# Moving a decoder's activation tiles and split weight buffers by some tens of columns in SBUF

## The chip, the cores and the metric

The kernel runs on one NeuronCore of a Trainium2 chip. The metric is the device time of one execution in microseconds (us), lower is better. Before the change it was 1270.6 us, the median of three runs (1267.6 to 1275.32).

## The reference

Three transformer blocks are computed on 256 tokens of width 1024, in float32. Cut to what matters:

```python
def first_block(x, mem, ...):
    for i in range(2):
        hn, mn = _rmsnorm(x, norm1[i]), _rmsnorm(mem, norm_mem[i])
        if i == 0: mix, q_mem = _nsa_mixer(hn, nsa_w_in, ...)      # sparse attention, 12 heads
        else:      mix, q_mem = _rwkv7_mixer(hn, rw_w_in, ...)     # recurrence over the tokens
        cross = _mem_attention(q_mem, mn, w_mem_kv[i])             # 256 memory rows
        x = x + jnp.concatenate([mix, cross], -1) @ w_o[i]
        x = x + _swiglu(_rmsnorm(x, norm2[i]), w_ffn_in[i], w_ffn_out[i])
    return _rmsnorm(x, final_norm)

def second_block(x, ...):
    proj = rmsnorm(x, mix_pre_g) @ w_in                            # 1024 -> 7176
    y_a = spatial_gating(...); y_b = forgetting_attention(...)
    x = x + rmsnorm((sigmoid(g_a) * y_a + sigmoid(g_b) * y_b) @ w_out, mix_post_g)
    return x + rmsnorm(swiglu(rmsnorm(x, ffn_pre_g), w_gate, w_up, w_down), ffn_post_g)
```

All weights together are some 180 MB, and each is used once.

## The kernel before

**Products.** Each large float32 product is made from three matmuls in the type float32r: both operands are split into a high part (`hi`) and the rest (`lo`), and `product` (L796) issues hi·hi (L798), then two mixed terms (L799, L800), into one PSUM bank. Each matmul loads its own stationary operand (LDWEIGHTS, the rows PEld) beside the matmul that runs before it.

**Weights.** SP loads them in pieces of 1024 columns by 256 outputs (2048 columns of 4 bytes in each of 128 partitions, `SLOT`) into a ring of three slots. ACT copies a piece into `w_hi` (L1622) and DVE writes the rest into `w_lo` (L2079). `w_hi` and `w_lo` have two slots each (`SPLITS`); piece number m goes to slot m mod 2. `split(name, k)` (L787) gives a piece's two views to PE. ACT fills a slot again when PE has done the piece before it there.

**Activations.** The normalised activations lie transposed, feature by token, in `act_hi` and `act_lo`, eight tiles of 256 tokens each (`KT` tiles of `S`). Together they are `fm` (L207). Every stage that begins with activations writes them into `fm` (`from_banks`, L1583 on ACT and L2036 on DVE) and reads them from there. The hidden layer of the three feed-forward parts has its own `hT_hi`, `hT_lo`, and the memory rows theirs (`mem_fm`, L285).

**Units.** PE goes through units in a fixed order. `fm_unit` (L802) has weights as the stationary operand and 256 tokens as the moving one; `tm_unit` (L821) has 128 tokens as the stationary operand and 256 columns of weights as the moving one; a full unit of either is 48 matmuls. `row_unit` (L850) has tokens as the stationary operand and 512 columns of weights as the moving one, 24 matmuls a piece. The stages, in order, with their matmuls through `product`:

| stage | what | units | matmuls |
|---|---|---|---|
| nsa | inputs of the sparse attention | q0 to qm0, most fm, two tm | 504 |
| mem | keys and values of the memory rows | kmem, vmem | 192 |
| wo0 | output projection | row | 96 |
| f0 | feed-forward: 22 fm units, then 11 row units on hT | f0_in, f0_out | 1056 + 264 |
| z | inputs of the recurrence | z0 to z10, qm1, fm | 552 |
| wo1, f1 | as wo0, f0 | | 96, 1056 + 264 |
| b2 | inputs of the second block | sv, fv, su, ga, gb are tm, fq, fk, sf fm | 1368 |
| wo2, f2 | as wo0, f0 | | 96, 1056 + 264 |

Between z and wo1 stands the recurrence itself (small matmuls of 64 by 64 in plain float32). There `cms` and `tt` (L311, L332) borrow the room of the activations, and `sc_parts`, `ems` (L294, L309) that of the split weights.

**Addresses.** `place` (L155) puts one tensor behind another, each start a multiple of 8 columns (a column is 4 bytes in each partition). `act_hi` begins at column 8192 and `act_lo` at 10240 of the kernel's room. The arena, which starts with `w_hi`, begins at column 24304. Since 16112 = 24304 − 8192 is 48 more than a multiple of 64, and all tile and slot sizes are multiples of 64, every tile of weights starts 48 columns (mod 64) behind every tile of activations. `hT` and the memory rows lie at a multiple of 64 from the weights.

```python
act_hi = place("act_hi", KT * S, dtype=F32R)             # L168
act_lo = place("act_lo", KT * S, dtype=F32R)             # L170
W_HI, W_LO = 0, SPLITS * SLOT                            # L192
fm = (tiles(act_hi), tiles(act_lo))                      # L207
pe.matmul(o, ahl[0], bhl[0], start=first, stop=False)    # L798
pe.matmul(o, ahl[0], bhl[1], start=False, stop=False)    # L799
return pe.matmul(o, ahl[1], bhl[0], start=False, stop=final)
```

Of the kernel before, what the change touches and what calls it, by code (L numbers as in the profile page):

```python
# [15 lines left out]
F32 = mybir.dt.float32  # L16
F32R = mybir.dt.float32r
# [119 lines left out]
def build(nc, T, out, ctx):  # L137
# [69 lines left out]
    fm = (tiles(act_hi), tiles(act_lo))  # L207
# [58 lines left out]
    arena_at[0] = MEM = (arena_at[0] + 7) // 8 * 8  # L266
# [27 lines left out]
    def score_parts(b):  # L294

        return [arena[:, o:o + n * 4 * CH].rearrange("p (u b t) -> p u b t", u=n, b=4)
                for o, n in ((W_HI + b * SLOT, 8), (W_LO + b * SLOT, 4))]
# [11 lines left out]
    ems = [arena[:, W_LO + (1 - EARLY_SLOT) * SLOT + (4 + gi) * 4 * CH:W_LO + (1 - EARLY_SLOT) * SLOT + (5 + gi) * 4 * CH]  # L309
           .rearrange("p (u t) -> p u t", u=4) for gi in range(3)]  # L310
    cms = place("cms", 3 * 4 * CH, ACT_HI - SHARED).rearrange("p (g u t) -> p g u t", g=3, u=4)  # L311
# [20 lines left out]
    tt = place("tt", 2 * H * CH, ACT_LO - SHARED).rearrange("p (r u t) -> p r u t", r=2, u=H)  # L332
# [447 lines left out]
    def _(pe):  # L780
# [208 lines left out]
        def ffn(tag):  # L989
            for j in range(FT):  # L990
                fm_unit(f"{tag}_in{j}", fm)
                if j == 0:
                    spread_scale(tag)
            for j in range(FT // 2):
                row_unit(f"{tag}_out", j, FT // 2, hT, hid_base[tag] + 2 * j + 2)

        def cross_product(step):

            qt, a, half = step // 4, step // 2 % 2, step % 2
            if step == 0:  # L1000
# [366 lines left out]
        for j in range(4):  # L1367
            row_unit("wo0_", j, 4, fm)
# [149 lines left out]
        for m, name in enumerate(FOX_FILL):  # L1518
# [3 lines left out]
            tm_unit(name, fm)  # L1522
# [16 lines left out]
    def _(act):  # L1539
# [64 lines left out]
        def split_to(end):  # L1604
            while split_at[0] < end:
# [7 lines left out]
                if new in MEM_UNITS:  # L1613
                    w = w_hi[:, (m % SPLITS) * SLOT:(m % SPLITS + 1) * SLOT].rearrange("p (k n) -> p k n", k=KT)
# [158 lines left out]
        from_banks([(fm, lambda k: ("norm1", k))])  # L1773
# [21 lines left out]
        from_banks([(fm, None)])  # L1795
# [3 lines left out]
        from_banks([(fm, lambda k: ("norm2", k))])  # L1799
# [5 lines left out]
        from_banks([(fm, lambda k: ("norm1", 8 + k))], 0)  # L1805
# [36 lines left out]
        act.activation(fm[0][:, 6:8, :], two("crT"), copy).then_inc(tick(own, "cross_hi"), 1)  # L1842
# [53 lines left out]
        from_banks([(fm, lambda k: ("norm2", 8 + k))], 0)  # L1896
# [6 lines left out]
        from_banks([(fm, lambda k: ("block2", k))], 0)  # L1903
# [51 lines left out]
        from_banks([(fm, None)])  # L1955
# [4 lines left out]
        from_banks([(fm, lambda k: ("ffn_pre_g_2", k))])  # L1960
# [7 lines left out]
    def _(dve):  # L1968
# [90 lines left out]
        def split_to(end):  # L2059
            while split_at[0] < end:  # L2060
# [4 lines left out]
                if new in MEM_UNITS:  # L2065
                    wh, wl = [w[:, (m % SPLITS) * SLOT:(m % SPLITS + 1) * SLOT].rearrange("p (k n) -> p k n", k=KT) for w in (w_hi, w_lo)]
# [123 lines left out]
        from_banks([(fm, lambda k: ("norm1", k))])  # L2190
# [179 lines left out]
        from_banks([(fm, lambda k: ("norm1", 8 + k))], 0)  # L2370
# [98 lines left out]
        dve.tensor_tensor(fm[1][:, 6:8, :], two("crT"), fm[0][:, 6:8, :].bitcast(F32),  # L2469
# [85 lines left out]
        def low_mix(j):  # L2555
# [3 lines left out]
            dve.tensor_tensor(fm[1][:, ts, :], mix_fm[:, ts, :], fm[0][:, ts, :].bitcast(F32),  # L2559
# [18 lines left out]
        from_banks([(fm, lambda k: ("norm2", 8 + k))], 0)  # L2578
# [8 lines left out]
        from_banks([(fm, lambda k: ("block2", k))], 0)  # L2587
# [136 lines left out]
        from_banks([(fm, None)])  # L2724
# [3 lines left out]
        from_banks([(fm, lambda k: ("ffn_pre_g_2", k))])  # L2728
# [36 lines left out]
```

## Time and profile before

| what | value |
|---|---|
| median of three runs | 1270.6 us (1267.6 to 1275.32) |
| the profiled execution's own time | 1267.52 us |
| its span, first to last instruction | 1265.7 us |
| PE busy | 1196.6 us, 95% |
| PE's weight loads busy | 1101.6 us, 87% |
| DVE busy | 763.1 us, 60% |
| ACT busy | 597.8 us, 47% |
| mean granted clock of TensorE | 0.971 of full speed |
| read from HBM | 181.90 MB, 145 GB/s over the span |

The span is 1.8 us shorter than the execution's own time. Matmuls are pipelined: a row gives 276 to 283 ns for one with 256 moving columns, while the next one starts some 115 ns after it. So the pace of PE is read from the distance between two starts, and a busy PE can be a PE at one of several paces.

### The profile page before, as it was taken

The page shows a single profiled execution, that of the slowest core. Times are in us where ns is not written, and L with a number is a line of the kernel's source. Part 1 is how long each engine was busy: PE and PEld are TensorE (multiplying, and loading weights), DVE is VectorE, ACT ScalarE, POOL GpSimd, SP SyncE. Part 2 cuts the span into 40 slices and gives each one's busy share as a digit, 9 for nine tenths or more (in the row PEclk, how much of TensorE's full clock was granted, in tenths as well). Part 3 has the DMA queues.
Part 4 walks back from the last instruction along what each step waited for, and adds up shares of the span by engine and source line. Part 5 has one row for each costly group of instructions (what it writes and reads, how often), then busy time and mean ns, then how long its engine had stood idle before and what let it go on. Part 6 is the DMA issues. An engine that isn't in the chain of part 4 may idle for free.

```text
span 1265.7 us, 24106 instructions
## 1 busy us (share of the span) xinstructions
PE 1196.6 (95%) x10320; PEld 1101.6 (87%) x10320; DVE 763.1 (60%) x1292; ACT 597.8 (47%) x1010; POOL 34.2 (3%) x39
## 2 busy tenths in 40 slices
PE   5999989999999998799899999999989988999997
PEld 5999878999988877799689998889978986999985
DVE  5565646677647667644666665475743666666644
ACT  4566545444434641333444444354347745444433
POOL 0000000000000102131000000000000000000000
PEclk9999989999999988899899999999989988999999
DMA  9822124867555431001268765636544343667551
GB/s 277 233 84 92 67 68 118 233 190 193 196 199 150 134 100 67 2 4 36 67 188 229 196 176 195 199 114 212 179 133 132 105 162 100 187 180 197 177 193 65
DMA packets 222694, 184.50 MB, mean 146 GB/s; under 512 B 19395, under 2 KB 208081, under 8 KB 222461
## 3 DMA queue, kind: packets, MB, share of 16 engines
q1 hardware_dynamic: 221386, 181.50, 47.9%
q8 instruction: 82, 1.34, 0.4%
q10 hardware_dynamic: 1202, 1.47, 0.4%
q14 instruction: 24, 0.19, 0.0%
HBM read 181.90 MB, written 1.05 MB: 145 GB/s over the span
## 4 chain that ended last, share of the span: by engine, by line
PE 83%; DVE 9%; ACT 3%; DMA 2%; issue 1%; SPq 1%; ACTq 0%; DVEq 0%
PE bank L798 23%; PE bank L799 22%; PE bank L800 22%; DVE w_lo L2079 3%; PE bank L1093 2%; PE bank L1314 1%; ACT w_hi L1622 1%; PE bank L1077 1%; PE bank L1298 1%; PE bank L1290 1%; DMA ring<-in_w_ffn_in 1%; SPq L739 1%; DMA ring<-in_nsa_w_in 1%; PE bank L942 1%; PE bank L946 1%
## 5 line engine op out<-in xcount | busy, mean ns | idle before, releaser
L2079 DVE TENSOR_TENSOR w_lo<-ring,w_hi 128x1024 fp32r<-128x1024 f32 x326 | 383.2, 1217 | 258.6 <-ACT w_hi L1622 258.4
L1622 ACT ACTIVATE w_hi<-ring 128x1024 fp32r<-128x1024 f32 x326 | 323.5, 1042 | 412.1 <-PE bank L800 394.6
L798 PE MATMUL bank<-act_hi,w_hi 128*128 128x256 f32 (+1 forms) x1512 | 427.4, 283 | 6.4 <-issue 3.4
L799 PE MATMUL bank<-act_lo,w_hi 128*128 128x256 f32 (+1 forms) x1512 | 423.6, 280 | 0.0
L800 PE MATMUL bank<-act_hi,w_lo 128*128 128x256 f32 (+1 forms) x1512 | 423.0, 280 | 0.0
L798 PEld LDWEIGHTS bank<-act_hi,w_hi 128*128 128x128 f32 (+1 forms) x1512 | 285.1, 189 | 10.9 <-issue 7.3
L799 PEld LDWEIGHTS bank<-act_lo,w_hi 128*128 128x128 f32 (+1 forms) x1512 | 284.7, 188 | 0.2
L800 PEld LDWEIGHTS bank<-act_hi,w_lo 128*128 128x128 f32 (+1 forms) x1512 | 284.6, 188 | 0.2
L798 PE MATMUL bank<-w_hi,act_hi 128*128 128x256 f32 (+1 forms) x448 | 141.3, 315 | 5.5 <-DVE act_lo L2047 2.5
L799 PE MATMUL bank<-w_lo,act_hi 128*128 128x256 f32 (+1 forms) x448 | 137.8, 308 | 0.0
L800 PE MATMUL bank<-w_hi,act_lo 128*128 128x256 f32 (+1 forms) x448 | 137.8, 308 | 0.0
L798 PE MATMUL bank<-w_hi,hT_hi 128*128 128x512 f32 x264 | 102.7, 389 | 0.0
L800 PE MATMUL bank<-w_hi,hT_lo 128*128 128x512 f32 x264 | 102.7, 389 | 0.0
L799 PE MATMUL bank<-w_lo,hT_hi 128*128 128x512 f32 x264 | 102.7, 389 | 0.0
L798 PEld LDWEIGHTS bank<-w_hi,act_hi 128*128 128x128 f32 x448 | 86.1, 192 | 15.1 <-issue 8.5
L2168 DVE TENSOR_TENSOR zshift<-bank,row_scale 128x512 f32<-128x512 f32 x66 | 45.7, 692 | 73.9 <-PE bank L800 73.8
L800 PEld LDWEIGHTS bank<-w_hi,act_lo 128*128 128x128 f32 x448 | 85.9, 192 | 4.9
L799 PEld LDWEIGHTS bank<-w_lo,act_hi 128*128 128x128 f32 x448 | 86.0, 192 | 4.6 <-issue 0.2
L800 PEld LDWEIGHTS bank<-w_hi,hT_lo 128*128 128x128 f32 x264 | 49.6, 188 | 10.4
L799 PEld LDWEIGHTS bank<-w_lo,hT_hi 128*128 128x128 f32 x264 | 49.5, 188 | 10.2
L798 PEld LDWEIGHTS bank<-w_hi,hT_hi 128*128 128x128 f32 x264 | 49.5, 188 | 10.1
L1627 ACT ACTIVATE arena<-bank 128x256 f32<-128x256 f32 (+4 forms) x59 | 24.6, 443 | 36.7 <-PE bank L1077 21.9
(315 smaller groups left out, 1288.5 us busy)
## 6 DMA issues: line engine op xcount, KB each, us to landing
ring<-in_w_ffn_in SPq DMA_DIRECT2D x88, 512.0 KB, 5.2
ring<-in_w_in SPq DMA_DIRECT2D x28, 1024.0 KB, 5.2
ring<-in_w_ffn_out SPq DMA_DIRECT2D x22, 1024.0 KB, 4.9
ring<-in_rw_w_in SPq DMA_DIRECT2D x11, 1024.0 KB, 5.2
ring<-in_w_gate SPq DMA_DIRECT2D x22, 512.0 KB, 4.0
ring<-in_w_up SPq DMA_DIRECT2D x22, 512.0 KB, 5.2
ring<-in_w_down SPq DMA_DIRECT2D x11, 1024.0 KB, 4.8
ring<-in_w_o SPq DMA_DIRECT2D x8, 1024.0 KB, 4.9
```

The lines of the kernel that those rows point to most:

```text
L739: sp.dma_start(dst, src).then_inc(slot_landed[r], 16)
L798: pe.matmul(o, ahl[0], bhl[0], start=first, stop=False)
L799: pe.matmul(o, ahl[0], bhl[1], start=False, stop=False)
L800: return pe.matmul(o, ahl[1], bhl[0], start=False, stop=final)
L942: ins = pe.matmul(score_bank(n)[:, c:c + nk], q[:, qt * P:(qt + 1) * P], k[:, 0:nk], start=True, stop=(kind != "fox"))
L946: ins = pe.matmul(score_bank(n)[:, c:c + nk], sel[0:NFH, i, :], ccum[0:NFH, 0:nk], start=False, stop=True)
L1077: ins = pe.matmul(bank_of(name)[half[q], a * CH:(a + 1) * CH], cms[gi][half[q], a, :], tms[gi][half[q], a, :], start=True, stop=True)
L1093: ins = pe.matmul(bank_of(name)[half[q], (4 * turned + a) * CH:(4 * turned + a + 1) * CH], left, right, start=True, stop=True)
L1622: act.activation(w_hi[:, (m % SPLITS) * SLOT + lo:(m % SPLITS) * SLOT + hi], ring[:, r * SLOT + lo:r * SLOT + hi], copy).then_inc(tick(own ...
L1627: act.activation(dst, bank_of(name)[:, :] if src is None else src, func, scale=scale).then_inc(freed(own, name), 1)
L2079: dve.tensor_tensor(w_lo[:, c], ring[:, r * SLOT + lo:r * SLOT + hi], w_hi[:, c].bitcast(F32), ALU.subtract).then_inc(tick(own, "lo_ready" ...
L2168: dve.tensor_tensor(scaled[:, j % 2, :].rearrange("p (b t) -> p b t", b=2), two(f"{tag}_in{j}"), scaled_pair(), ALU.mult).then_inc(freed(o ...
```

## The change

- `act_hi` and `act_lo` become one tensor `act_pair` of 2·2048 + 56 columns. Each stage gets a home, a number of columns by which both its tiles are shifted: nsa 40, wo0 0, f0 48, z 4, wo1 0, f1 24, b2 16, wo2 0, f2 56. `fm` becomes `fm_of[stage]` wherever it is written or read.
- The start of the arena is filled up to a multiple of 64 columns from `ACT_HI`. The tensors between the activations and the arena move by 56 columns, the arena by 80.
- The two slots of `w_hi` and of `w_lo` lie 2056 columns apart instead of 2048 (`PITCH`, 32 bytes more). `w_lo` starts at the next multiple of 64.
- The memory rows start at a multiple of 64 plus 16 columns (64 bytes) instead of at a multiple of 8.
- Nothing else is changed: no instruction is added, removed or put in another place, and no wait is.

```diff
-    ACT_HI = fixed_at[0]
-    act_hi = place("act_hi", KT * S, dtype=F32R)
-    ACT_LO = fixed_at[0]
-    act_lo = place("act_lo", KT * S, dtype=F32R)
+    LINES, ROOM = 64, 56
+    ACT_HI = fixed_at[0]
+    act_pair = place("act_pair", 2 * KT * S + ROOM, dtype=F32R)
+    ACT_LO = ACT_HI + KT * S
...
+    fixed_at[0] += (ACT_HI - fixed_at[0]) % LINES
     SHARED = fixed_at[0]
-    ARENA = 28672
+    ARENA = 28800
...
-    W_HI, W_LO = 0, SPLITS * SLOT
-    w_hi = place("w_hi", SPLITS * SLOT, W_HI, F32R)
-    w_lo = place("w_lo", SPLITS * SLOT, W_LO, F32R)
-    FREE = 2 * SPLITS * SLOT
+    PITCH = SLOT + 8
+    W_HI, W_LO = 0, (SPLITS * PITCH + LINES - 1) // LINES * LINES
+    w_hi = place("w_hi", SPLITS * PITCH, W_HI, F32R)
+    w_lo = place("w_lo", SPLITS * PITCH, W_LO, F32R)
+    FREE = 2 * W_LO
...
-    fm = (tiles(act_hi), tiles(act_lo))
+    HOMES = {"nsa": 40, "wo0": 0, "f0": 48, "z": 4, "wo1": 0, "f1": 24, "b2": 16, "wo2": 0, "f2": 56}
+
+    def home(name):
+
+        return tuple(tiles(act_pair[:, i * KT * S + HOMES[name]:(i + 1) * KT * S + HOMES[name]]) for i in range(2))
+
+    fm_of = {name: home(name) for name in HOMES}
...
-    arena_at[0] = MEM = (arena_at[0] + 7) // 8 * 8
+    arena_at[0] = MEM = (arena_at[0] + LINES - 1) // LINES * LINES + 16
...
-            return [w[:, b * SLOT:b * SLOT + n].rearrange("p (k n) -> p k n", k=k) for w in (w_hi, w_lo)]
+            return [w[:, b * PITCH:b * PITCH + n].rearrange("p (k n) -> p k n", k=k) for w in (w_hi, w_lo)]
...
         def ffn(tag):
             for j in range(FT):
-                fm_unit(f"{tag}_in{j}", fm)
+                fm_unit(f"{tag}_in{j}", fm_of[tag])
```

The other lines of the diff put `PITCH` for `SLOT` where ACT and DVE write a split piece and where `sc_parts` and `ems` lie, and `fm_of[...]` for `fm`; `cms` and `tt` stay at home 0 (wo1's).

## Rows read from the trace of the kernel before

**Rows 1.** page, span and part 1 (busy us, share, instructions)

```profile
span 1265.7 us, 24106 instructions
...
PE 1196.6 (95%) x10320; PEld 1101.6 (87%) x10320; DVE 763.1 (60%) x1292; ACT 597.8 (47%) x1010; POOL 34.2 (3%) x39
```

**Rows 2.** page, part 4, the chain that ended last, by engine

```profile
PE 83%; DVE 9%; ACT 3%; DMA 2%; issue 1%; SPq 1%; ACTq 0%; DVEq 0%
```

**Rows 3.** groups by line and form, PE, whole span (busy us, mean ns)

```profile
L798 PE MATMUL bank<-act_hi,w_hi 128*128 128x256 f32 x1496 | 422.9, 283 | 6.4 <-issue 3.4 <-DVE act_lo L2049 1.7 <-DVE w_lo L2079 1.2
```

**Rows 4.** timeline of PE, f0_in1's first matmul and f0_out0's first (start us, us)

```profile
218.45 0.36 PE L798 MATMUL bank<-act_hi,w_hi 128*128 128x256 f32 x1
...
332.78 0.39 PE L798 MATMUL bank<-w_hi,hT_hi 128*128 128x512 f32 x1
```

**Rows 5.** timeline of PE, the same two places of stage f1, then of f2

```profile
650.90 0.36 PE L798 MATMUL bank<-act_hi,w_hi 128*128 128x256 f32 x1
...
770.59 0.40 PE L798 MATMUL bank<-w_hi,hT_hi 128*128 128x512 f32 x1
...
1077.53 0.36 PE L798 MATMUL bank<-act_hi,w_hi 128*128 128x256 f32 x1
...
1196.33 0.39 PE L798 MATMUL bank<-w_hi,hT_hi 128*128 128x512 f32 x1
```

**Rows 6.** timeline of PE, inside unit kmem0, memory rows as the moving operand

```profile
110.61 0.28 PE L798 MATMUL bank<-mem_hi,w_hi 128*128 128x256 f32 x1
...
111.33 0.28 PE L798 MATMUL bank<-mem_hi,w_hi 128*128 128x256 f32 x1
```

**Rows 7.** timeline of PE, inside unit qm0, then inside z9

```profile
100.80 0.28 PE L798 MATMUL bank<-act_hi,w_hi 128*128 128x256 f32 x1
...
103.16 0.28 PE L800 MATMUL bank<-act_hi,w_lo 128*128 128x256 f32 x1
...
396.30 0.28 PE L800 MATMUL bank<-act_hi,w_lo 128*128 128x256 f32 x1
...
396.65 0.28 PE L800 MATMUL bank<-act_hi,w_lo 128*128 128x256 f32 x1
```

**Rows 8.** timeline of PE, block 2, last matmuls of fk3 and first of fv0

```profile
905.16 0.28 PE L799 MATMUL bank<-act_lo,w_hi 128*128 128x256 f32 x1
...
906.81 0.28 PE L798 MATMUL bank<-w_hi,act_hi 128*128 128x256 f32 x1
...
908.06 0.28 PE L800 MATMUL bank<-w_hi,act_lo 128*128 128x256 f32 x1
```

**Rows 9.** timeline of PE, inside unit sf, whose weight loads have 8 columns

```profile
858.88 0.28 PE L800 MATMUL bank<-act_hi,w_lo 128*8 128x256 f32 x1
...
861.27 0.28 PE L800 MATMUL bank<-act_hi,w_lo 128*8 128x256 f32 x1
```

**Rows 10.** timeline of PE, inside wo0, then inside f0_out

```profile
196.71 0.39 PE L800 MATMUL bank<-w_hi,act_lo 128*128 128x512 f32 x1
...
198.34 0.39 PE L798 MATMUL bank<-w_hi,act_hi 128*128 128x512 f32 x1
...
339.83 0.39 PE L799 MATMUL bank<-w_lo,hT_hi 128*128 128x512 f32 x1
...
341.42 0.39 PE L800 MATMUL bank<-w_hi,hT_lo 128*128 128x512 f32 x1
```

**Rows 11.** stretches, inside f0: PE, PEld, DVE, ACT, POOL busy, PEclk, DMA, GB/s

```profile
240.00:280.00 40.00, 40.00 (x356) 40.00 (x355) 27.68 (x37) 19.72 (x30) 0.00 (x0) 1.00 0.73 200
```

**Rows 12.** chain of waits in order of time, around f1's start

```profile
654.32 11.94 DMA ring<-in_w_ffn_in
```

**Rows 13.** groups of PE's instructions by line and form, matmuls in plain f32

```profile
L1093 PE MATMUL bank<-tt,arena 64*64 64x64 f32 x480 | 20.4, 220 | 1.4 <-DVE tt L2522 1.0 <-issue 0.2
...
L942 PE MATMUL bank<-arena 128*128 128x256 f32 x16 | 6.1, 466 | 0.0
...
L1207 PE MATMUL bank<-arena,cst 128*128 128x256 f32 x16 | 3.9, 383 | 0.0
```

More of the change, by code:

```diff
@@ L296, in score_parts @@
         return [arena[:, o:o + n * 4 * CH].rearrange("p (u b t) -> p u b t", u=n, b=4)
-                for o, n in ((W_HI + b * SLOT, 8), (W_LO + b * SLOT, 4))]
+                for o, n in ((W_HI + b * PITCH, 8), (W_LO + b * PITCH, 4))]
     sc_parts = [score_parts(EARLY_SLOT), score_parts(1 - EARLY_SLOT)]
@@ L307, in sc @@
         return part[:, us.start - first:us.stop - first]
-    ems = [arena[:, W_LO + (1 - EARLY_SLOT) * SLOT + (4 + gi) * 4 * CH:W_LO + (1 - EARLY_SLOT) * SLOT + (5 + gi) * 4 * CH]
+    ems = [arena[:, W_LO + (1 - EARLY_SLOT) * PITCH + (4 + gi) * 4 * CH:W_LO + (1 - EARLY_SLOT) * PITCH + (5 + gi) * 4 * CH]
            .rearrange("p (u t) -> p u t", u=4) for gi in range(3)]
-    cms = place("cms", 3 * 4 * CH, ACT_HI - SHARED).rearrange("p (g u t) -> p g u t", g=3, u=4)
+    cms = place("cms", 3 * 4 * CH, ACT_HI + HOMES["wo1"] - SHARED).rearrange("p (g u t) -> p g u t", g=3, u=4)
     cms = [cms[:, gi] for gi in range(3)]
@@ L331, in build @@
     assert arena_at[0] <= AFTER + 3 * NT * S + 3 * S
-    tt = place("tt", 2 * H * CH, ACT_LO - SHARED).rearrange("p (r u t) -> p r u t", r=2, u=H)
+    tt = place("tt", 2 * H * CH, ACT_LO + HOMES["wo1"] - SHARED).rearrange("p (r u t) -> p r u t", r=2, u=H)
     tt = [tt[:, pr] for pr in range(2)]
@@ L1006, in cross_product @@
             k = 6 + a
-            ins = product(bank_of("wo1_3", 2 * qt + half)[:, :], [v[:, k, qt * P:(qt + 1) * P] for v in fm],
+            ins = product(bank_of("wo1_3", 2 * qt + half)[:, :], [v[:, k, qt * P:(qt + 1) * P] for v in fm_of["wo1"]],
                           [v[:, a, half * 512:(half + 1) * 512] for v in split("wo1_3", 2)], a == 0, False)
@@ L1320, in fill @@
             name = FILL[s]
-            act = mem_fm if name in MEM_UNITS else fm
+            act = mem_fm if name in MEM_UNITS else fm_of["nsa"]
             (tm_unit if name in ("vw", "vmem0", "vmem1") else fm_unit)(name, act, half)
@@ L1367, in _ @@
         for j in range(4):
-            row_unit("wo0_", j, 4, fm)
+            row_unit("wo0_", j, 4, fm_of["wo0"])
         residual_to_fm(4, lambda i: evacuated("wo0_0", i))
@@ L1621, in split_to @@
                 for lo, hi in pieces(new):
-                    act.activation(w_hi[:, (m % SPLITS) * SLOT + lo:(m % SPLITS) * SLOT + hi],
+                    act.activation(w_hi[:, (m % SPLITS) * PITCH + lo:(m % SPLITS) * PITCH + hi],
                                    ring[:, r * SLOT + lo:r * SLOT + hi], copy).then_inc(tick(own, "hi_ready"), 1)
@@ L1772, in _ @@
         act.wait_ge(sem("tables"), 1)
-        from_banks([(fm, lambda k: ("norm1", k))])
+        from_banks([(fm_of["nsa"], lambda k: ("norm1", k))])
         ahead("q0")
@@ L1794, in _ @@
             step_end(s)
-        from_banks([(fm, None)])
+        from_banks([(fm_of["wo0"], None)])
         rows_ahead("wo0")
@@ L1841, in _ @@
         act.wait_ge(*filled("crT"))
-        act.activation(fm[0][:, 6:8, :], two("crT"), copy).then_inc(tick(own, "cross_hi"), 1)
+        act.activation(fm_of["wo1"][0][:, 6:8, :], two("crT"), copy).then_inc(tick(own, "cross_hi"), 1)
         def act_hop(hop, c):
@@ L1891, in _ @@
             act.wait_ge(sem("mix1_ready"), j + 1)
-            act.activation(fm[0][:, 2 * j:2 * j + 2, :], mix_fm[:, 2 * j:2 * j + 2, :], copy).then_inc(tick(own, "mix1_hi"), 1)
+            act.activation(fm_of["wo1"][0][:, 2 * j:2 * j + 2, :], mix_fm[:, 2 * j:2 * j + 2, :], copy).then_inc(tick(own, "mix1_hi"), 1)
         ahead("wo1_0"), ahead("wo1_1")
@@ L2189, in _ @@
         split_to(1)
-        from_banks([(fm, lambda k: ("norm1", k))])
+        from_banks([(fm_of["nsa"], lambda k: ("norm1", k))])
         def lay_blocks(v):
@@ L2359, in _ @@
         dve.wait_ge(*last(own))
-        from_banks([(fm, None)])
+        from_banks([(fm_of["wo0"], None)])
         rows_ahead("wo0")
         residual("wo0_0", "wo0_3")
-        from_banks([(fm, lambda k: ("norm2", k))])
+        from_banks([(fm_of["f0"], lambda k: ("norm2", k))])
         mean_square(2, x_tm)
@@ L2468, in _ @@
         dve.wait_ge(sem("cross_hi"), 1)
-        dve.tensor_tensor(fm[1][:, 6:8, :], two("crT"), fm[0][:, 6:8, :].bitcast(F32),
+        dve.tensor_tensor(fm_of["wo1"][1][:, 6:8, :], two("crT"), fm_of["wo1"][0][:, 6:8, :].bitcast(F32),
                           ALU.subtract).then_inc(freed(own, "crT"), 1)
```

66 lines of the change are left out of this document (33 added, 33 removed).

## The prediction

> **What bounds the kernel now.** I read the page first, then the groups by form, then the timeline of PE at chosen places. The page says that PE is busy for 1196.6 of 1265.7 us [rows 1], and the chain that ended last is PE's for 83% [rows 2]. So time is won where PE goes faster, or nowhere: no edit here takes an instruction out. The groups by form show that the great mass of it is one shape, activations against weights with 256 moving columns: L798 alone has 1496 of them in the fm form, at a mean of 283 ns each [rows 3]. That duration says little, since matmuls overlap. What counts is how far apart two starts are, and the timeline gives that.
>
> **The paces.** In f0 the first matmul of unit 1 starts at 218.45 and the first of the output part at 332.78 [rows 4]. Between them lie 21 units of 48 matmuls, so 114.33 us / 1008 = **113.4 ns**. The same work, with the same addresses, takes 1196.33 − 1077.53 = 118.80 us in f2 (117.9 ns) and 119.69 us in f1, part of it short pauses [rows 5]. So one and the same sequence has two paces, 113.4 and some 118 ns. Elsewhere:
> - memory rows, 6 steps in 0.72 us: 120 ns [rows 6];
> - nsa, 20 steps in 2.36 us: 118.0 ns; z, 3 steps in 0.35 us: 117 ns [rows 7];
> - block 2: 14 steps in 1.65 us, 117.9 ns, up to the first matmul of fv0, then 11 steps in 1.25 us, 113.6 ns, with no pause between [rows 8]. At that place the operands change sides: the weights are moved and the tokens are stationary from there on;
> - sf, whose weight loads have 8 columns instead of 128: 21 steps in 2.39 us, 113.8 ns [rows 9];
> - 512 moving columns: 7 steps in 1.63 us, 233 ns, in wo0, against 7 steps in 1.59 us, 227 ns, in f0_out [rows 10]. The same weights slots are read, but the stationary operand is `act` in the one and `hT` in the other.
>
> I take two things from this. **113.4 ns (227 for 512 columns) is the floor of the stream**, since a load sixteen times shorter does not go below it [rows 9]. And what is added to the floor, 4.5 ns, 6.6 ns or 6 ns a matmul, hangs on which two operands are read at the same time. As a matmul streams one operand, the load for the next one reads the other. I count by D, the start of the stationary operand less that of the moving one, in columns modulo 64, worked out from the placements in the code. Before: fm units 48, tm units and wo 16, memory and hT 0. So D = 0 gave 120 ns with 256 columns and the floor with 512; D = 16 gave 233 ns with 512 and the floor in fv0; D = 48 gave both paces. Position matters, and it is not all: f0 and f2 have the same D.
>
> **The change, part by part.** Nothing is issued anew, so there are no terms but the pace. With h for a stage's home and b for the slot (0 or 1), D becomes 8b − h in fm units and h − 8b in tm units, and alternates from piece to piece: nsa 24/32 (tm 40/32), f0 16/24, z 60/4, f1 40/48, b2 48/56 (tm 16/8), f2 8/16, wo and outputs 0/56, memory 48/56 (tm 16/8). What the slow paces cost now, over the floor:
> - f2: 118.80 − 114.33 = 4.5 us over 21 units, 4.6 with the first [rows 4, 5];
> - f1: the same pace, 4.6 us; the rest of its 119.69 are waits, which stay [rows 4, 5];
> - nsa: 504 matmuls, some 430 of them following closely, × 4.5 ns = 1.9 us; z: some 500 of 552 × 4.4 = 2.2 us [rows 7];
> - b2: 1368 matmuls, of which I take 45% at the slow pace as in the units up to fk3, × 4.4 = 2.8 us [rows 8];
> - memory: 170 of 192 × 6.6 ns = 1.1 us [rows 6]; wo: 288, less some that wait, × 6 ns = 1.6 us [rows 10].
>
> The sum is **18.8 us**, and that is the most that can be won: f0 and the outputs are at the floor and can only lose. The rows have no price for most of the new D; each is bounded by the floor below and by D = 0's 6.6 ns above. For f1 and f2, the long stretches, I take the floor, 9.2 us, because two of the three distances seen have reached it at 256 columns (D = 48 in f0, D = 16 in fv0) and nothing in these stages breaks the stream. For the short stages I take half of 9.6, so 4.8. Slot 1 of the outputs moves from D = 0 to 56: between nothing and 396 × 6 ns = 2.4 us; I take nothing. A faster PE needs its pieces sooner. f0 shows that it gets them: at the fast pace PE is busy for all of 40.00 us, with DVE at 27.68, ACT at 19.72 and 200 GB/s [rows 11]. Where it waits in any case nothing is won, as at f1's start, where the chain has 11.94 us of a weight transfer [rows 12]; for this I take off 1 us. **9.2 + 4.8 − 1 = 13 us.**
>
> The plain f32 matmuls see new distances too. The 64 × 64 ones of the recurrence go from D = 48 and 16 to 0 between `tt` and the arena, and have 220 ns now [rows 13]. With 256 columns in plain f32 a matmul at D = 0 has 466 ns (L942) where one at 54 has 383 (L1207) [rows 13], so this can cost: L1093 has 480 records in 20.4 us of PE, 43 ns each [rows 13], and a tenth more on all 864 of the line, an estimate between nothing and those 22%, would be 3.7 us. I take nothing, since chains of DVE and ACT stand between them, and keep it for the upper end.
>
> One rule speaks against all this. The Trainium skill, page "SBUF — State Buffer", section "Who interferes with whom", gives PE two independent read ports, one for the moving operand and one for weight loads, and says that PE never waits on anyone. By it homes would be worth 0 us and the sum would be 1270.6. The trace agrees in part only: equal shapes run at 113.4, 118 and 120 ns [rows 4 to 7], but f0 and f2 differ at equal addresses.
>
> **Rivals.**
> - *The entry decides, not the distance.* f0, f1 and f2 are alike in every address and two are slow [rows 4, 5]; so the pace may be set by the moment at which a stretch starts and then hold. Then the change deals the paces anew: perhaps f0 slow and f2 fast, net about nothing, **1270.6** (1265 to 1277). Against it: wo and hT, memory and act differ in every unit [rows 6, 7, 10].
> - *Positions do nothing.* The two reads may never meet, and the paces may come from what DVE and ACT do beside a unit. Then every stage keeps its pace and the time stays at **1270.6**, within the scatter of 3. For it: f0 and f2 again. Against it: DVE and ACT have the same work beside f0 and f2, since the units are the same, and fv0 changed its pace without a pause [rows 8]. The page named above would have it so.
> - *New collisions.* The new D of the long stages may be of the bad kind, as D = 0 is at 256 columns. It would show first in f0: 1056 × 4.5 = 4.8 us more, or 7 at 120 ns. With block 2 slow throughout (750 × 4.4 = 3.3) and slot 1 of the outputs at 233 (2.4), and f1 and f2 unchanged, that is + 10.5, so **1281**. It decides where f0 and b2 lose more than f1 and f2 gain. For it: nothing shows that D = 24, 40 or 56 is good. Against: D = 16 and 48 are among the new ones.
>
> **The numbers.** The profiled execution had 1267.52 us, 3.1 below the median of 1270.6; the sum is a difference, so I take it from the median: 1270.6 − 13 = **1257.6**. Chances: distances help 0.65, entry decides 0.17, positions do nothing 0.08, new collisions 0.10. The range goes down to the full 18.8 and the runs' scatter of 3 (1270.6 − 21.8 = 1249) and up to where the two cases around 1270.6 mostly end, 1273. A measurement tells about 0.5% (6.4 us) from no change: below 1264.2 is faster, above 1277 slower. Of the first case 0.04 ends within 0.5%; of the second 0.04 is faster and 0.02 slower. So faster 0.65, same 0.04 + 0.11 + 0.08 = 0.23, slower 0.12. Most of the range is on one side, so it needs no second one.
>
> **What would show it.** Right: f1 and f2 take some 114.5 us from their second unit to their output part, f0 stays at 114.3, and matmuls there show 276 ns. Memory units show 113 to 118 ns between starts, wo 227 in at least one slot. DVE, ACT and DMA keep their busy times. Wrong: f0 at 118 ns, a pace that changes from piece to piece with the slot, hT outputs above 227 ns in every second piece, or a wkv stretch whose L1093 starts lie further apart.

## The result and the profile after

The changed kernel takes 1277.32 us (median of 18 runs, 1271.41 to 1281.64) against 1271.18 us for the kernel before (18 runs, 1265.26 to 1275.32). The ratio is 1.0045, with a 95% interval of 1.003 to 1.0059. The forecast was 1257.6 us, in a range that ended at 1273. So the change made the kernel 6 us slower, where I had it 13 us faster.

The page of the changed kernel, span and part 1, beside [rows 1]:

```profile
span 1276.2 us, 24106 instructions
...
PE 1207.1 (95%) x10320; PEld 1109.7 (87%) x10320; DVE 762.8 (60%) x1292; ACT 598.7 (47%) x1010; POOL 34.2 (3%) x39
```

PE is busy for 10.5 us more, with the same 10320 matmuls, and the span is 10.5 us longer. DVE (762.8) and ACT (598.7) are where they were. So the time is lost in PE's own work, most of it in the pace of the products. The timeline of PE shows how. These are the first matmuls of f0_in18 to f0_in21, then those of f0_out0 to f0_out2 (columns: start us, us):

```profile
317.48 0.28 PE L807 MATMUL bank<-act_pair,w_hi 128*128 128x256 f32 x1
...
323.24 0.28 PE L807 MATMUL bank<-act_pair,w_hi 128*128 128x256 f32 x1
...
328.69 0.28 PE L807 MATMUL bank<-act_pair,w_hi 128*128 128x256 f32 x1
...
334.45 0.28 PE L807 MATMUL bank<-act_pair,w_hi 128*128 128x256 f32 x1
...
339.90 0.39 PE L807 MATMUL bank<-w_hi,hT_hi 128*128 128x512 f32 x1
...
345.50 0.40 PE L807 MATMUL bank<-w_hi,hT_hi 128*128 128x512 f32 x1
...
350.98 0.40 PE L807 MATMUL bank<-w_hi,hT_hi 128*128 128x512 f32 x1
```

Every second unit is slow. Units of 256 columns take 5.76 us, 5.45 us, 5.76 us, 5.45 us, that is 120.0 and 113.5 ns for each of their 48 matmuls, where the kernel before had 113.4 throughout [rows 4]. Output units take 5.60 and 5.48 us where 24 matmuls at 227 ns need 5.44 [rows 10]. The slow pieces are those of slot 1, which the change put 8 columns further. In f1 and f2 (f1_in18 and f1_in19, then f2_in17 to f2_in19):

```profile
757.00 0.28 PE L807 MATMUL bank<-act_pair,w_hi 128*128 128x256 f32 x1
...
762.76 0.28 PE L807 MATMUL bank<-act_pair,w_hi 128*128 128x256 f32 x1
...
1178.08 0.28 PE L807 MATMUL bank<-act_pair,w_hi 128*128 128x256 f32 x1
...
1183.52 0.28 PE L807 MATMUL bank<-act_pair,w_hi 128*128 128x256 f32 x1
...
1189.20 0.28 PE L807 MATMUL bank<-act_pair,w_hi 128*128 128x256 f32 x1
```

f1_in18 takes 5.76 us, and in f2 the units take 5.44 and 5.68 us: there one slot did win, and reached the floor of 113.3 ns that f2 did not have before [rows 5].

I went through all starts in both traces and summed, stage by stage, what closely following matmuls take over 113.33 and 226.67 ns. Before it is 19.2 us, after 25.6 us. The difference of 6.4 us (entries are rounded one by one):

| stage | over the floor, before | after | difference |
|---|---|---|---|
| f0, input units | 0.2 | 3.6 | + 3.4 |
| outputs of f0, f1, f2 | 0.1 | 3.2 | + 3.1 |
| f1, input units | 4.7 | 5.8 | + 1.1 |
| f2, input units | 4.6 | 2.6 | − 2.0 |
| b2 | 2.8 | 4.7 | + 1.9 |
| nsa | 1.9 | 2.2 | + 0.3 |
| memory rows, wo, z | 4.9 | 3.6 | − 1.4 |

That lies close to the medians' 6.1 us, but in part by luck: a second trace of the kernel before, shown below, has 23.2 us over the floor, 2.4 less than the changed kernel's, since its f0 ran slow. How the paces fell in the executions without a trace is not known. The two profiled executions lie 10.5 us apart, and some 3.5 us of this is not the pace of products: TensorE's granted clock fell to its lower level (1.2 of 2.4 GHz) for a longer part of the 70 us around the memory rows in the one trace than in the other. These 70 us (PE, PEld, DVE, ACT, POOL busy, PEclk, DMA share, GB/s), first the kernel before, then the changed one:

```profile
120.00:190.00 70.00, 64.77 (x463) 57.83 (x462) 41.41 (x146) 37.42 (x110) 0.00 (x0) 0.88 0.19 61
```

```profile
120.00:190.00 70.00, 63.94 (x448) 57.66 (x447) 40.50 (x144) 37.09 (x110) 0.00 (x0) 0.83 0.20 62
```

With half speed at the lower level, a mean of 0.83 over 70 us is 2 x 0.17 x 70 = 24 us there, and 0.88 is 17. This points to the executions and not to the change: the mean granted clock is 0.969 over the 18 executions of the changed kernel and also over 18 of the kernel before. With both terms the account closes: from each of the fourteen traces' spans, take what the products spend over the floor and half of the time at the lower clock, and 1205 to 1214 us are left, 1209 and 1208 for the two of the kernel before and 1208 for the changed one.

### The profile page after: what moved, and what is told of

Same layout as the page of the kernel before. It is cut to its first block, busy times and chain, and to the rows that moved or that the text cites. A ratio compares the mean times of both kernels' runs of the same rounds, so it can differ in the third digit from the quotient of the medians.

```text
span 1276.2 us, 24106 instructions
## 1 busy us (share of the span) xinstructions
PE 1207.1 (95%) x10320; PEld 1109.7 (87%) x10320; DVE 762.8 (60%) x1292; ACT 598.7 (47%) x1010; POOL 34.2 (3%) x39
## 4 chain that ended last, share of the span: by engine, by line
PE 82%; DVE 9%; ACT 4%; DMA 2%; issue 1%; SPq 1%; ACTq 0%; DVEq 0%
PE bank L807 23%; PE bank L808 22%; PE bank L809 22%; DVE w_lo L2088 3%; PE bank L1102 2%; PE bank L1323 1%; ACT w_hi L1631 1%; PE bank L1086 1%; DMA ring<-in_w_ffn_in 1%; SPq L748 1%; PE bank L1307 1%; PE bank L1299 1%; DMA ring<-in_nsa_w_in 1%; PE bank L951 1%; PE bank L955 1%
## 5 line engine op out<-in xcount | busy, mean ns | idle before, releaser
L807 PE MATMUL bank<-act_pair,w_hi 128*128 128x256 f32 (+1 forms) x1512 | 429.0, 284 | 5.7 <-issue 3.4
L808 PE MATMUL bank<-act_pair,w_hi 128*128 128x256 f32 (+1 forms) x1512 | 425.4, 281 | 0.0
L809 PE MATMUL bank<-act_pair,w_lo 128*128 128x256 f32 (+1 forms) x1512 | 425.3, 281 | 0.0
L807 PEld LDWEIGHTS bank<-act_pair,w_hi 128*128 128x128 f32 (+1 forms) x1512 | 286.7, 190 | 9.9 <-issue 7.5
L808 PEld LDWEIGHTS bank<-act_pair,w_hi 128*128 128x128 f32 (+1 forms) x1512 | 286.2, 189 | 0.3
L809 PEld LDWEIGHTS bank<-act_pair,w_lo 128*128 128x128 f32 (+1 forms) x1512 | 286.1, 189 | 0.3
L807 PE MATMUL bank<-w_hi,act_pair 128*128 128x256 f32 (+1 forms) x448 | 141.8, 317 | 5.2 <-DVE act_pair L2056 2.5
L808 PE MATMUL bank<-w_lo,act_pair 128*128 128x256 f32 (+1 forms) x448 | 138.6, 309 | 0.0
L809 PE MATMUL bank<-w_hi,act_pair 128*128 128x256 f32 (+1 forms) x448 | 138.2, 309 | 0.0
L807 PEld LDWEIGHTS bank<-w_hi,act_pair 128*128 128x128 f32 x448 | 86.4, 193 | 14.6 <-issue 8.4
L809 PEld LDWEIGHTS bank<-w_hi,act_pair 128*128 128x128 f32 x448 | 86.1, 192 | 4.7
L808 PEld LDWEIGHTS bank<-w_lo,act_pair 128*128 128x128 f32 x448 | 86.2, 192 | 4.3 <-issue 0.2
```

## The experiments

Two theories stood after the first look. **Distance**: the pace hangs on D, the start of the operand that is loaded less that of the operand that streams, in columns mod 64. **Entry**: f0 and f2 had the same D before and different paces, so the pace is dealt when a stretch begins. Twelve runs were made, ten of new kernels and two of kernels that had run already.

### The kernel before, once more

> The kernel before once more. Distance theory: in this kernel every fm unit has D = 48, which leaves two paces open, so f1, f2, z and nsa show some 118 ns again, and f0 shows 113.4 or 118 ns: it has no price for which. Entry theory: the pace of a stretch is dealt anew in each execution, so at least one of f0, f1, f2 changes its pace against the first trace.

One execution took 1271.63 us. The first matmul of f0_in1 and that of f0_out0:

```profile
220.02 0.36 PE L798 MATMUL bank<-act_hi,w_hi 128*128 128x256 f32 x1
...
338.82 0.39 PE L798 MATMUL bank<-w_hi,hT_hi 128*128 128x512 f32 x1
```

118.80 us for the 1008 matmuls that had taken 114.33 [rows 4]. The program and its addresses are the same, and f0 runs at 117.9 ns this time. f1 and f2 are at 117.9 again. So at D = 48 there are two paces, and the execution picks. My first trace had caught f0 on its good side. This alone is worth 4.5 us, and the two executions lie 4.1 us apart. That much of the other runs' scatter comes from it is likely, but only traced executions could show it.

### The slots' pitch undone

```diff
-    PITCH = SLOT + 8
+    PITCH = SLOT
```

> The changed kernel with the two weight slots a slot's size apart again (PITCH = SLOT), homes and memory rows as changed. Distance theory: D is now the same in both slots: nsa 24, f0 16, z 60, f1 40, b2 48 (tm 16), f2 8, wo and outputs 0. So f0 goes to 113.4 ns in every unit (3.4 us won against the changed kernel), the outputs and wo to 227 ns (3.1 us + 0.5 won), b2 back to the kernel before (1.9 won), f1 to 120 ns (1 lost), f2 to 118.4 ns (2.6 lost): some 1271, that is 6 us below the changed kernel. Entry theory: paces are dealt anew, no unit pattern follows the slots in either kernel, 1277 within 5 us.

1270.74 us, ratio to before 0.9989 (0.9972 to 1.0006). The forecast of 1271 held. f0_in1 and f0_out0, f1_in2 and f1_out0, f2_in2 and f2_out0:

```profile
220.79 0.36 PE L807 MATMUL bank<-act_pair,w_hi 128*128 128x256 f32 x1
...
335.13 0.39 PE L807 MATMUL bank<-w_hi,hT_hi 128*128 128x512 f32 x1
...
653.35 0.29 PE L807 MATMUL bank<-act_pair,w_hi 128*128 128x256 f32 x1
...
768.55 0.40 PE L807 MATMUL bank<-w_hi,hT_hi 128*128 128x512 f32 x1
...
1080.75 0.28 PE L807 MATMUL bank<-act_pair,w_hi 128*128 128x256 f32 x1
...
1194.35 0.39 PE L807 MATMUL bank<-w_hi,hT_hi 128*128 128x512 f32 x1
```

f0 (D = 16) takes 114.34 us, the floor. Over 20 units f1 (D = 40) takes 115.20 us, 120.0 ns, and f2 (D = 8) 113.60 us, 118.3 ns. All outputs are at 226.7 ns. So the homes by themselves win nothing and lose nothing: f1 and f2 went to distances at which no trace has shown a fast pace (3 us more than in the first trace of before), and what wo, z and the memory rows won (2.8 us) made up for it.

### The pitch alone

```diff
-    HOMES = {"nsa": 40, "wo0": 0, "f0": 48, "z": 4, ...}
+    HOMES = {"nsa": 16, "wo0": 16, "f0": 16, "z": 16, ...}   # 16 in all nine
-    arena_at[0] = MEM = (arena_at[0] + LINES - 1) // LINES * LINES + 16
+    arena_at[0] = MEM = (arena_at[0] + LINES - 1) // LINES * LINES + 0
```

> Only the slots' pitch of the change: home 16 in all stages and the memory rows at a multiple of 64, so that slot 0 has the kernel before's distances (fm 48, tm and wo 16, outputs and memory 0), and slot 1 lies 8 columns further. Distance theory: slot 1 outputs at 234 ns (396 x 7 = 2.8 us more, less some), slot 1 fm units at D = 56 and tm units at D = 8 at 117 to 120 ns, none of them at 113: against the kernel before f0 and b2 lose 2 to 4 us, in all 5 to 7 us slower, 1277. If the homes were to blame and not the pitch: 1271.

1276.18 us, ratio 1.0054 (1.0033 to 1.0075), within 1.2 us of the whole change. f0_in18 to f0_in20, then f0_out0 to f0_out2:

```profile
313.88 0.28 PE L807 MATMUL bank<-act_pair,w_hi 128*128 128x256 f32 x1
...
319.48 0.28 PE L807 MATMUL bank<-act_pair,w_hi 128*128 128x256 f32 x1
...
324.92 0.28 PE L807 MATMUL bank<-act_pair,w_hi 128*128 128x256 f32 x1
...
335.96 0.40 PE L807 MATMUL bank<-w_hi,hT_hi 128*128 128x512 f32 x1
...
341.55 0.39 PE L807 MATMUL bank<-w_hi,hT_hi 128*128 128x512 f32 x1
...
347.02 0.40 PE L807 MATMUL bank<-w_hi,hT_hi 128*128 128x512 f32 x1
```

Slot 1 (D = 56) takes 5.60 us where slot 0 (D = 48) takes 5.44, and the outputs 5.59 and 5.47. One thing I had not expected: in f0 and f1 every unit of slot 0 came out at 113 ns, in f2 every one at 118, both behind units at D = 56. The outputs (3.1 us), b2 (1.6) and f0 (1.6) lose, while f1 wins 2.7 in this trace, which is that of the fastest of the six executions (1274.4).

### One term alone: the outputs' pieces level again

```diff
+    def slot_at(m):
+        return (m % SPLITS) * (SLOT if "_out" in split_names[m] else PITCH)
...
-            return [w[:, b * PITCH:b * PITCH + n].rearrange("p (k n) -> p k n", k=k) for w in (w_hi, w_lo)]
+            return [w[:, o:o + n].rearrange("p (k n) -> p k n", k=k) for w in (w_hi, w_lo)]
```

> The changed kernel with one part undone: the pieces of the three output parts (f0_out, f1_out, f2_out) lie a slot's size apart again, so D = 0 in all of them; everything else, D = 56 in the wo units of slot 1 included, is as changed. Distance theory: all outputs at 227 ns, 396 matmuls x 6.7 ns and what spills over = 3.1 us below the changed kernel's 1277.3, so 1274 (ratio to before 1.002), and the input parts of f0, f1, f2 keep their pattern of 113 and 117 to 120 ns. Entry theory: outputs as before anyway, no more than 1 us won.

1274.79 us, ratio 1.0031 (1.0014 to 1.0048). By the medians that is 2.5 us below the changed kernel, by the ratios 1.8, and the two intervals overlap, so the total alone doesn't prove the gain; the trace shows it directly. f0_out0 and f0_out10:

```profile
339.15 0.39 PE L810 MATMUL bank<-w_hi,hT_hi 128*128 128x512 f32 x1
...
393.56 0.39 PE L810 MATMUL bank<-w_hi,hT_hi 128*128 128x512 f32 x1
```

Ten units take 54.41 us, 226.7 ns a matmul. The input parts of f0 and f2 keep the changed kernel's times to 0.01 us (117.67 and 116.74). This is the term that the prediction had priced and then set to nothing.

### Two maps of D

One run shows several distances when only the homes differ. The edits are against the changed kernel, the first map's homes above the second's; both have the pitch of `SLOT`, and the first has `ROOM` 64 for its home 60:

```diff
-    PITCH = SLOT + 8
+    PITCH = SLOT
...
-    HOMES = {"nsa": 40, "wo0": 0, "f0": 48, "z": 4, "wo1": 0, "f1": 24, "b2": 16, "wo2": 0, "f2": 56}
+    HOMES = {"nsa": 60, "wo0": 0, "f0": 8, "z": 0, "wo1": 0, "f1": 40, "b2": 16, "wo2": 0, "f2": 32}
```

```diff
+    HOMES = {"nsa": 56, "wo0": 0, "f0": 46, "z": 47, "wo1": 0, "f1": 44, "b2": 16, "wo2": 0, "f2": 52}
```

> A map: PITCH = SLOT and homes nsa 60, f0 8, z 0, f1 40, f2 32, which give D = 4, 56, 0, 24, 32 in the fm units. Distance theory: the two odd multiples of 8 (f0 at D = 56, f1 at 24) show 117 to 120 ns, as D = 24 had 119.9 in the changed kernel's f0; D = 0 in z shows 120 ns as the memory rows had; D = 32 and D = 4 are open. Entry theory: the paces are 113.4 or 118 ns and nothing else, whatever D is.

> A finer map: PITCH = SLOT and homes nsa 56, f0 46, z 47, f1 44, f2 52, which give D = 8, 18, 17, 20, 12 in the fm units. If a column of 4 bytes counts, D = 17 and 18 show paces of their own, between those of 16 and 24. If only the 64 bytes line (16 columns) counts, D = 17 to 20 and 12 all show the slow pace of D = 24 or 8, 117 to 120 ns. If pieces of 8 columns count, D = 17 to 20 show the 113 or 118 ns of D = 16.

1275.38 and 1280.37 us, one execution each. f0_in2 and f0_out0, in the first map (D = 56) and in the second (D = 18):

```profile
226.06 0.28 PE L807 MATMUL bank<-act_pair,w_hi 128*128 128x256 f32 x1
...
338.06 0.40 PE L807 MATMUL bank<-w_hi,hT_hi 128*128 128x512 f32 x1
```

```profile
227.22 0.28 PE L807 MATMUL bank<-act_pair,w_hi 128*128 128x256 f32 x1
...
342.42 0.40 PE L807 MATMUL bank<-w_hi,hT_hi 128*128 128x512 f32 x1
```

112.00 us for 960 matmuls is 116.7 ns, 115.20 us is 120.0. By the same reckoning, over all kernels, for 256 moving columns (most distances were seen in one or two executions):

| D | ns from start to start |
|---|---|
| 16, 48 | 113.3 to 113.5 or 117.7 to 117.9 |
| 56 | 116.7 and 117.7 |
| 4, 60 (stage z) | 117.2; 115.8 to 117.2 |
| 17 (z), 24, 32 | 118.6; 117.3 to 119.9; 118.7 |
| 8, 12, 20 | 118.3; 119.2; 119.3 |
| 0, 18, 40 | 119.4 to 120; 120.0; 120.0 |

For 512 columns: 226.7 at D = 0, 233 at 8, 16 and 56. In the fm units of the long stages the floor was seen at 16 and 48 alone. Two columns past 16, at 18, a whole stage ran as slow as any, so 8 bytes count, and "the same 32 bytes piece" is not the rule. That paces of 113 or 118 and nothing else occur, as the entry theory alone would have it, is wrong too. That D repeats after 64 columns is assumed: within a unit the operands' blocks lie 128 and 256 columns apart at one pace, but no run compares D and D + 64.

### The distance or the place

```diff
-    fixed_at[0] += (ACT_HI - fixed_at[0]) % LINES
+    fixed_at[0] += (ACT_HI - fixed_at[0]) % LINES + 8
...
-    PITCH = SLOT + 8
+    PITCH = SLOT
...
-    HOMES = {"nsa": 40, "wo0": 0, "f0": 48, "z": 4, "wo1": 0, "f1": 24, "b2": 16, "wo2": 0, "f2": 56}
+    HOMES = {"nsa": 56, "wo0": 8, "f0": 56, "z": 56, "wo1": 8, "f1": 56, "b2": 24, "wo2": 8, "f2": 56}
```

> The d16 kernel with all four kinds of operand (activations, split weights, hT, memory rows) 8 columns (32 bytes) further, so that every distance is d16's and every start is 8 past a multiple of 16 columns. If the distance alone counts: 227 ns in outputs and wo, 113.4 or 118 ns in the fm units at D = 16, as in d16. If a start that isn't at a multiple of 64 bytes costs by itself: 231 to 235 ns in every output unit, 117 to 120 ns in every fm unit.

1265.9 us. d16 (below) with every operand 8 columns further: homes 8 more, the start of the arena 8 more. f2_in19 and f2_in20, then f0_out0 and f0_out1:

```profile
1178.39 0.28 PE L807 MATMUL bank<-act_pair,w_hi 128*128 128x256 f32 x1
...
1183.83 0.28 PE L807 MATMUL bank<-act_pair,w_hi 128*128 128x256 f32 x1
...
338.75 0.39 PE L807 MATMUL bank<-w_hi,hT_hi 128*128 128x512 f32 x1
...
344.19 0.39 PE L807 MATMUL bank<-w_hi,hT_hi 128*128 128x512 f32 x1
```

5.44 us each: the floor, at starts that are 32 bytes off a multiple of 64. f0 is at 118 ns and f1 at 118 from its fifth unit. For this one shift it is the distance that counts, not the place.

### All fm stages at D = 16

```diff
-    PITCH = SLOT + 8
+    PITCH = SLOT
...
-    HOMES = {"nsa": 40, "wo0": 0, "f0": 48, "z": 4, "wo1": 0, "f1": 24, "b2": 16, "wo2": 0, "f2": 56}
+    HOMES = {"nsa": 48, "wo0": 0, "f0": 48, "z": 48, "wo1": 0, "f1": 48, "b2": 16, "wo2": 0, "f2": 48}
```

> PITCH = SLOT and home 48 in nsa, f0, z, f1, f2, 16 in b2, 0 in the wo stages: D = 16 in all fm units but those of b2, D = 16 in b2's tm units, D = 0 with 512 columns. Distance theory: 113.4 ns in f0, z, f1, f2 and nsa, 227 ns in wo and outputs; against the kernel before 4.6 + 4.6 + 2 + 1.7 + 1.5 + 0.6 = 15 us won, so 1256 (ratio 0.988). Entry theory: some stage of these is at 118 ns again, 1266 to 1275. Positions do nothing: 1271.

1264.49 us, ratio 0.9939 (0.9914 to 0.9963): 0.6% faster than the kernel before, but 8 us short of the distance theory's 1256. f2_in1 and f2_out0, then f1_in2, f1_in3, f1_in5 and f1_in6:

```profile
1075.18 0.36 PE L807 MATMUL bank<-act_pair,w_hi 128*128 128x256 f32 x1
...
1193.98 0.40 PE L807 MATMUL bank<-w_hi,hT_hi 128*128 128x512 f32 x1
...
654.38 0.28 PE L807 MATMUL bank<-act_pair,w_hi 128*128 128x256 f32 x1
...
659.82 0.28 PE L807 MATMUL bank<-act_pair,w_hi 128*128 128x256 f32 x1
...
672.40 0.28 PE L807 MATMUL bank<-act_pair,w_hi 128*128 128x256 f32 x1
...
678.05 0.28 PE L807 MATMUL bank<-act_pair,w_hi 128*128 128x256 f32 x1
```

f2 took 118.80 us, the slow pace from its second unit to its last. f1 had units of 5.44 us and, from its fifth on, units of 5.65. In between lies f1_in3 with a start 6.85 us before the next one's, a wait of 1.2 us for `w_lo` of DVE. So D = 16 has the same two paces as D = 48, a pace holds while nothing interrupts the stream, and an interruption can change it. Each theory alone is wrong. Together they fit what was seen: **the distance sets which paces are open, the entry picks among them**.

### A distance for every piece

The pieces get offsets of their own in their slots, so that D = 16 in all units of 256 columns, tm units and memory rows too, and D = 0 in all of 512.

```diff
-    PITCH = SLOT + 8
+    PITCH = SLOT + 64
...
+        if kind.endswith("_out"):
+            o = 40
+        elif kind.startswith("wo"):
+            o = 16
+        elif kind in ("vs", "vw", "vmem", "sv", "su", "fv", "ga", "gb"):
+            o = 0
+        else:
+            o = 32
```

All homes are 0, and the arena is not aligned, so that it lies 48 behind the activations as before; hT lies at 40 in it.

> Every piece of weights gets an offset of its own in its slot, by what reads it: 16 columns behind the activations in fm units, 16 ahead of them in tm units, level with them in the wo units and with hT in the outputs. So D = 16 in every product with 256 columns, D = 0 with 512. Distance theory alone: 113.4 and 227 ns everywhere, 19 us below the kernel before, 1252. Distance and entry together (D = 16 allows 113.4 and 118 ns, the entry picks): 227 ns in all units of 512, a mixture of 113 and 118 in the others that holds from unit to unit, 1257 to 1268. Entry alone: 1271.

1256.2 us (7 runs, 1252.11 to 1269.0), ratio 0.9911 (0.9877 to 0.9944). f2_in1 and f2_out0:

```profile
1069.10 0.37 PE L824 MATMUL bank<-act_pair,w_hi 128*128 128x256 f32 x1
...
1183.44 0.39 PE L824 MATMUL bank<-w_hi,hT_hi 128*128 128x512 f32 x1
```

f2 has the floor, 114.34 us, and f0 too; f1 fell to 118 ns after its wait, as in d16. What is left over the floor is 8.9 us, against 19.2 in the first trace of the kernel before. The median flatters: the mean of the seven is 1259.2, and by the ratio 11 us are won, not 14. The same kernel once more:

> The placed kernel once more, as it was. Distance and entry together: the same two paces in the units of 256 and nothing else, 227 ns in those of 512, but at least one of f0, f1, f2, z, b2 holds another pace for some stretch than in the first trace, since its execution enters at another moment. If the program alone decided, every unit would show its pace of the first trace again.

1256.55 us. f0_in1 and f0_out0 lie 114.34 us apart again and f2's 114.35, so those stages did not move. f1_in1 and f1_in2, and the first trace's, in this order:

```profile
647.30 0.37 PE L824 MATMUL bank<-act_pair,w_hi 128*128 128x256 f32 x1
...
653.04 0.28 PE L824 MATMUL bank<-act_pair,w_hi 128*128 128x256 f32 x1
```

```profile
645.25 0.36 PE L824 MATMUL bank<-act_pair,w_hi 128*128 128x256 f32 x1
...
650.79 0.28 PE L824 MATMUL bank<-act_pair,w_hi 128*128 128x256 f32 x1
```

5.74 against 5.54 us: here f1 was slow from its first units on. The paces of z and nsa fell otherwise too. Some of the seven executions of `placed` had 1264 and 1269 us; they have no trace.

There is one more kind of entry, with no gap at all. Between fk3 and fv0 the operands change sides. In the first trace of `placed` the first matmuls of fk3, fv0 and the unit behind it are:

```profile
894.13 0.28 PE L824 MATMUL bank<-act_pair,w_hi 128*128 128x256 f32 x1
...
899.58 0.28 PE L824 MATMUL bank<-w_hi,act_pair 128*128 128x256 f32 x1
...
905.23 0.28 PE L824 MATMUL bank<-w_hi,act_pair 128*128 128x256 f32 x1
```

fk3 takes 5.45 us and fv0 5.65 us, both at D = 16. All four traces of `placed` and its kicked forms (below) have this. In the ten other traces it is the other way round: fk3, at D = 48 or 56, takes 5.65 us, and fv0, at D = 16, 5.45. So a change of sides can change the pace too, in both directions. Apart from it, in none of the fourteen traces does a stretch at D = 16 or 48 change its pace without a step of more than 125 ns before it.

### Can the fast pace be asked for?

In the changed kernel each unit of f0 at D = 16 came behind one at 24, and each ended at 113 ns. So I put some pieces 8 columns further, as a kick.

The edit is a tuple of names against `placed`, to whose offsets 8 is added (`kick` first, then `kick3`):

```diff
-    KICK = ()
+    KICK = ('f0_in0', 'f0_in4', 'f1_in0', 'f1_in4', 'f1_in8', 'f2_in0', 'f2_in4', 'z9', 'z3', 'z0', 'z6')
```

```diff
+    KICK = ('f0_in1', 'f1_in4', 'f2_in1')
```

> As placed, and the pieces of eleven fm units (f0_in0, f0_in4, f1_in0, f1_in4, f1_in8, f2_in0, f2_in4, z9, z3, z0, z6) lie 8 columns further, at D = 24, so that the unit behind each enters D = 16 from D = 24. Distance and entry together: in the changed kernel each of 11 entries of this kind in f0 ended at 113 ns, so all units of f0, f1 and f2 but the seven are at 113 (9 us below the kernel before in f1 and f2, 3 more in z, nsa, memory rows and wo), seven units at 120 ns cost 0.3 us each: some 1258, and below placed if placed has slow stages. Distance alone: slower than placed by 11 x 0.3 = 3 us. Entry alone: 1271.

> As placed, with only three pieces 8 columns further: f0_in1, f1_in4, f2_in1. Distance and entry together: the units behind each stay at 113 ns to the end of their stage; three units at 120 ns cost 1 us, and f1, slow in placed's trace from its fifth unit, gains 3.9 less that. So 1255 to 1258, with less scatter between executions than placed (1252 to 1269). If D = 24 does not lead into the fast pace: as placed, with the same scatter, and a stage at 118 ns behind a kicked unit.

`kick`: 1259.74 us (1256.43 to 1262.93), ratio 0.9913 (0.9892 to 0.9934). `kick3`: 1259.88 us (1256.59 to 1265.71), ratio 0.9924 (0.9897 to 0.9951). Neither differs from `placed` beyond its interval. In kick3, f0_in1 and f0_out0, then f1_in4, f1_in5 and f1_in6:

```profile
222.28 0.36 PE L824 MATMUL bank<-act_pair,w_hi 128*128 128x256 f32 x1
...
341.06 0.40 PE L824 MATMUL bank<-w_hi,hT_hi 128*128 128x512 f32 x1
...
672.96 0.36 PE L824 MATMUL bank<-act_pair,w_hi 128*128 128x256 f32 x1
...
678.73 0.28 PE L824 MATMUL bank<-act_pair,w_hi 128*128 128x256 f32 x1
...
684.18 0.28 PE L824 MATMUL bank<-act_pair,w_hi 128*128 128x256 f32 x1
```

f1's kicked unit took 5.77 us, the next 5.45, and f1 stayed at 113 ns to its end, which no kernel had whose f1 lay at D = 16 or 48 throughout. But in f0 the kicked unit was followed by 5.65 us units to the end: 118.78 us. Behind a kicked unit 113 ns followed in f1 and f2 of `kick3` and in f0, f1 and f2 of `kick`; in kick3's f0 it did not, and in z of `kick` not throughout. So the trace of `kick` has the least over the floor of all, 6.6 us, and still its execution took 1256.43 us where that of `placed`, with 2 us more, took 1254.63: the rest of an execution varies by as much. The expectation that D = 24 always leads to the fast pace is wrong. What picks the pace at an entry stays open.

## Why the prediction was wrong

- *PE's pace bounds the kernel; the floor is 113.4 and 227 ns.* Right. No kernel went below it, and in the changed kernel DVE and ACT kept their busy times to 1 us. The most that could be won, 18.8 us, fits the 19.2 counted in that trace (its term for block 2 is 2.7 by its own factors, not 2.8); in the second trace of the same kernel it was 23.2. `placed` has 8.9 left.
- *"For f1 and f2 … I take the floor, 9.2 us, because two of the three distances seen have reached it."* **This step failed.** Those two were 16 and 48. Of the new ones in f1 and f2, D = 8 and 40 showed no fast pace (118.3 and 120.0 ns), nor did 24 in f0 (119.9), and f1's 48 held its slow one. f1 lost 1.1 us, and f2 won 2.0, in the slot that had D = 16. I had a scale of "between the floor and 120" for each new distance and chose the floor, with no row for it. My own rows had D = 48 at 118 ns in f1 and f2, so a distance seen at the floor once was no promise. The other of the two, D = 16 in fv0, was read right behind a change of sides, where the pace can change at one and the same distance: in `placed` fv0 took the slow pace at D = 16. Instead of 9.2 us, f1 and f2 together won 0.9 in the traces, and that f2's D = 16 came out fast was the entry's luck: in `d16` all of f2 was slow at D = 16.
- *"f0 and the outputs are at the floor and can only lose"*: right, and then I let them lose nothing. Slot 1 of f0 went to D = 24 and cost 3.4 us. "Slot 1 of the outputs moves from D = 0 to 56: between nothing and 2.4 us; I take nothing": it measured 3.1 us in the trace, and 2.5 us by the medians when undone alone. The nearest row was wo0's 233 ns, with which I had priced it.
- *Block 2, expected to win its half of 2.8 us, lost 1.9*: slot 1 went from D = 16 to D = 8 in its tm units (118.3 ns).
- *Half of the short stages*: memory rows won 0.6 and wo 0.5 of the 2.7 at stake, z 0.3, and nsa lost 0.3. In all, of the 13 us forecast 8.3 are missing in f1 and f2, 6.5 in f0 and the outputs, and 3.3 in block 2.
- *Rivals.* "New collisions", chance 0.10, had the mechanism and the places, f0, b2 and outputs; its 1281 was 4 us too high, since f0 and block 2 lost 1.4 us less each than it said and f2 won. "The entry decides" holds as one half of the truth, shown by the kernel before itself. "Positions do nothing" falls: in `pitch_back` 1008 such matmuls took 114.34 us in f0 at D = 16 and 121.03 in f1 at D = 40, pauses of some 0.2 us included, where the slow pace at 16 or 48 takes 118.80. In f0 itself, 960 took 115.20 us at D = 18. The Trainium skill, page "SBUF — State Buffer", section "Who interferes with whom", has PE wait on nobody; as far as it concerns PE's own two reads, these runs do not agree.
- *Plain f32 matmuls at D = 0 in the recurrence*, kept for the upper end: that group (L1093, L1102 after) kept its 20.4 us of PE and its 220 ns each, and its closely following starts (837 steps, each below 0.2 us) add up to 25.0 us before and after. It cost nothing.
- One of my signs of being wrong, a pace that changes from piece to piece with the slot, is what the profile showed.

## What to carry to other kernels

When PE streams without a gap, measure from start to start, not by an instruction's duration, and compare the same work in several stages: a step of 4 or 6 ns on every matmul is visible there and nowhere else. If it is there, give each pair of operands (what streams, and what is loaded meanwhile) a distance that the trace has shown at the floor, and change nothing that already has one: a single pitch moved all pieces of one slot, the good ones too. Look at more than one execution before pricing a pace, since one distance can hold two.

## What was not expected of the hardware

- In this kernel a stream of float32r matmuls has discrete paces that can last for a whole stage. At D = 16 and 48 there were two, 113.4 and 117.8 ns, with the same program and addresses; a unit of 48 matmuls takes 5.44 or 5.65 us, and f0 of the kernel before took 114.33 us in one execution and 118.80 in another.
- The paces react to single columns: 113.4 or 117.8 ns at D = 16, 118.6 at 17 (stage z) and 120.0 at 18 (f0), the last two in one execution each.
- 32 bytes between two slots cost 0.54% of the kernel (ratio 1.0054, 1.0033 to 1.0075), with no instruction changed.
- The distances that are good for 256 columns are not those for 512: D = 0 gave 120 ns in the one and the floor of 226.7 in the other; D = 16 gave 113.4 and 233.
